# PLE gate matrix through the weight ring in place of a resident copy, with eleven row slots and three sum buffers

## What is computed

```python
for i in range(DEPTH):                    # DEPTH = 1
    ...
    h = h + merged @ w_out[i]
    h = h + peer_ffn(rms_norm(h, norm_ffn[i]), peer_wq[i], peer_keys[i], peer_u[i], peer_v[i])
    h = h + jax.nn.sigmoid(rms_norm(h, norm_ple[i]) @ ple_gate[i]) * (p[i] @ ple_proj[i])
```

## Time and profile before

| | us |
|---|---|
| three runs, median | 3986.89 |
| lowest and highest | 3982.22, 3993.07 |
| profiled execution | 3986.96 |
| its span in the profile | 3984.8 |
| PE busy in the span | 3115.6 (78%) |
| DVE busy | 2691.8 (68%) |
| ACT busy | 1377.4 (35%) |
| POOL busy | 1225.4 (31%) |

### The profile page before, as it was taken

How to read it: one execution, slowest core, us unless ns; L and a number is a source line. 1 busy time by engine, 2 the same in 40 slices (tenths; PEclk the granted TensorE clock), 3 DMA queues, 4 the chain that set the end, 5 groups by cost and what they waited for, 6 DMA issues and landing times. The chain is left out here.

```text
span 3984.8 us, 31095 instructions
## 1 busy us (share of the span) xinstructions
PE 3115.6 (78%) x7816; PEld 1412.6 (35%) x7816; DVE 2691.8 (68%) x5254; ACT 1377.4 (35%) x3574; POOL 1225.4 (31%) x1092
## 2 busy tenths in 40 slices
PE   8979999897889989878777877888765656556656
PEld 4545555543434434433333332333322222222222
DVE  3345545312477767777778777868888887888884
ACT  3213333202344344334333423343333334334332
POOL 0000000000233324433344343434444444444442
PEclk9988898798999999989889998889888878878887
DMA  4330101255899999999999999999999999999996
GB/s 160 118 141 24 44 29 37 97 209 222 349 393 414 393 360 421 418 418 378 417 398 417 361 393 391 426 355 411 424 412 399 424 419 389 420 414 393 426 422 265
DMA packets 212916, 1295.14 MB, mean 325 GB/s; under 512 B 24608, under 2 KB 38176, under 8 KB 69408
## 3 DMA queue, kind: packets, MB, share of 16 engines
q0 software_dynamic: 147456, 1073.81, 65.5%
q1 hardware_dynamic: 59552, 207.15, 13.8%
q10 hardware_dynamic: 5760, 12.59, 0.8%
HBM read 1253.60 MB, written 39.85 MB: 325 GB/s over the span
## 5 line engine op out<-in xcount | busy, mean ns | idle before, releaser
L1297 PE MATMUL l_acc<-l_rows,l_diag 128*128 128x512 f32 x2560 | 1422.6, 698 | 732.0 <-ACT l_diag L1431 718.4
L1198 POOL DMA_INDIRECT l_rows<-in_peer_uv,l_at x1024 | 1189.6, 1162 | 1732.1 <-DVE l_acc L1577 1082.3
L1567 DVE SCALAR_TENSOR_TENSOR l_rows<-l_rows,l_xn 128x1024 f32<-128x1024 f32 x1024 | 1227.1, 1224 | 320.2 <-DMA l_rows<-in_peer_uv,l_at 259.8
L1297 PEld LDWEIGHTS l_acc<-l_rows,l_diag 128*128 128x128 f32 x2560 | 526.2, 218 | 1563.6 <-ACT l_diag L1431 1025.8
L1577 DVE SCALAR_TENSOR_TENSOR l_acc<-l_rows,l_wts,l_acc 128x1024 f32<-128x1024 f32 x384 | 492.6, 1283 | 135.0 <-ACT l_wts L1427 135.0
L1423 ACT ACTIVATE l_dots<-l_dots 128x2 f32<-128x2 f32 x512 | 103.8, 203 | 1080.8 <-DVE l_rows L1567 1076.0
L1191 POOL CAST l_at<-l_expert 128x16 uint32<-128x16 f32 x64 | 35.7, 557 | 978.8 <-DVE l_expert L1553 978.5
L117 PE MATMUL l_pa<-all_ring,l_xt 128*128 128x512 f32 x656 | 296.9, 604 | 17.6 <-DMA l_xt<-kept_xnt 17.2
L117 PE MATMUL l_pa<-l_ring,l_xt 128*128 128x512 f32 x624 | 285.1, 608 | 18.2 <-DMA l_xt<-kept_xnt 12.3
L1427 ACT ACTIVATE l_wts<-l_dots,l_gates 128x1 f32<-128x1 f32 x1024 | 293.5, 287 | 16.8
L1431 ACT ACTIVATE l_diag<-all_ident,l_wts 128x128 f32<-128x128 f32 x640 | 257.1, 402 | 21.0
(11 more groups left out here) (241 smaller groups left out, 2780.4 us busy)
## 6 DMA issues: line engine op xcount, KB each, us to landing
l_ring<-in_w_late SPq DMA_DIRECT2D x44, 1024.0 KB
all_ring<-in_w_late SPq DMA_DIRECT2D x44, 1024.0 KB
l_rows<-in_peer_uv,l_at POOLq DMA_INDIRECT x1024
l_yt<-kept_yt SPq DMA_DIRECT2D x48, 256.0 KB, 12.4
kept_s<-l_yt ACTq DMA_DIRECT2D x32, 256.0 KB
l_s_in<-kept_s SPq DMA_DIRECT2D x64, 128.0 KB
mix_w_branches<-in_w_branches_kept SPq DMA_DIRECT2D x8, 768.0 KB, 4.5
kept_yt<-b_yt SPq DMA_DIRECT2D x8, 768.0 KB
```

The lines of the kernel that those rows point to most:

```text
L1198: pool.indirect_dma_start(out=rows[:, r % SLOTS, :], out_offset=None, in_=A["peer_uv"], in_offset=bass.IndirectOffsetOnAxis(ap=at[:, c % 2 ...
L1297: ins = pe.matmul(acc2[:, hs], diag[n_pe(r) % DIAGS][:], rows[:, r % SLOTS, D + half * HB:D + (half + 1) * HB], start=first, stop=last)
L1567: dve.scalar_tensor_tensor(out=u, in0=u, scalar=1.0, in1=xn[:, t % 2, :], op0=ALU.mult, op1=ALU.mult, accum_out=dots[:, n:n + 1]).then_inc ...
```

## The change

`SLOTS` goes from 8 to 11, `acc` from 2 to 3 buffers (`ACCS`), and the resident `wg` goes. In SBUF, 32 KB of each partition are given up, and 3 x 8 + 4 = 28 KB are taken. The gate matrix is appended to `w_late` as chunks 30 to 33 (two for each half), and is taken twice through the ring: once for tiles 0 and 1, between group 1 and group 2, and once for tiles 2 to 7, behind group 2. Group 2's jobs start at slot 64 x 2 + 6 = 134 rather than at 104, with the same due slot. PLE of tile t can't stand before the queries of the groups that precede its chunks (plus 4), nor before the PLE of tile t - 1 is over.

```diff
-SLOTS = 8
+SLOTS = 11
...
+ACCS = 3
+PLE_TILES = ((0, 1), (2, 3, 4, 5, 6, 7))
...
-        for g in range(len(GROUPS)):
-            self.group(g)
+        self.group(0)
+        self.group(1)
+        self.ple(PLE_TILES[0])
+        self.group(2)
+        self.ple(PLE_TILES[1])
         self.place()
-        self.ple()
...
-            begin = end
+            begin = self.first + len(PLE_TILES[0]) * NSEL // 2 + 6
         for job in rest:
+            if job.g == 2:
+                at = max(at, float(begin))
...
+    def ple(self, tiles):
+
+        c = self.take("w_late", 30, 31, 32, 33)
+        for t in tiles:
+            self.add((t,), "hturn", 1.8, pb=2, t=t)
+            for half in range(2):
+                self.add((t, half), "pgate", 6.9, pa=1, chunk=c + 2 * half, n_chunks=2, t=t, half=half)
+
+    def place_ple(self):
+
+        free = 0
         for t in range(T):
...
+            queries = [job.slot for job in self.jobs if job.kind == "query" and job.g <= (t not in PLE_TILES[0]) + 1]
+            slot = max(self.first + (t + 1) * NSEL // 2, max(queries) + 4, free)
+            self.of["hturn", t].slot = slot + 1
+            for half in range(2):
+                self.of["pgate", t, half].slot = slot + 3 + half
+            free = slot + 6
...
-        wg = sb("wg", [P, DC, D])
...
-        xn, acc = sb("xn", [P, 2, D]), sb("acc", [P, 2, D])
+        xn, acc = sb("xn", [P, 2, D]), sb("acc", [P, ACCS, D])
...
-                wait(sp, out_done, (t - 1) * 16)
-                sp.dma_start(acc[:, t % 2, :], X["h"][t]).then_inc(acc_in[t % 2], 16)
+                wait(sp, out_done, (t - ACCS + 1) * 16)
+                sp.dma_start(acc[:, t % ACCS, :], X["h"][t]).then_inc(acc_in[t % ACCS], 16)
...
-                if s == 8:
-                    sp.dma_start(wg[:], A["ple_gate"]).then_inc(wg_in, 16)
...
-                    if s == max(stored, plan.first - 1 if t < 2 else plan.first + (t - 1) * NSEL // 2 + 9):
+                    given = plan.of["pgate", t - ACCS, 1].slot + 4 if t >= ACCS else 0
+                    if s == max(stored, plan.first - 1 if t < 2 else plan.first + (t - 1) * NSEL // 2 + 9, given):
                         load_h(t)
...
-                    after = s - plan.first - (t + 1) * NSEL // 2
-                    if after == 4:
+                    if s == plan.of["pgate", t, 1].slot:
                         load_pp(t)
-                    if after == 7:
+                    if s == plan.of["pgate", t, 1].slot + 3:
                         store_tile(t)
...
-                if job.t == 0:
-                    pe.wait_ge(wg_in, 16)
+                loaded(pe, job.chunk)
+                loaded(pe, job.chunk + 1)
...
-                hs = slice(job.half * HB, (job.half + 1) * HB)
-                matmuls(pe, into_pa(job.pa[0])[:], [(ht[:, c * P:(c + 1) * P], wg[:, c, hs]) for c in range(DC)]).then_inc(pa_done, 1)
+                matmuls(pe, into_pa(job.pa[0])[:], [(ht[:, c * P:(c + 1) * P], wide_chunk(job.chunk, c)) for c in range(DC)]).then_inc(pa_done, 1)
```

More of the change, by code:

```diff
@@ L912, in place @@
         slot, used = 0, 0.0
-        jobs = iter(self.jobs)
+        jobs = iter([job for job in self.jobs if job.t is None])
         start = self.of["score", 0, 1]
@@ L940, in place @@
         self.n_slots = self.end + 10
-    def ple(self):
-        for t in range(T):
[L945 to L948, removed]
+        self.place_ple()
+    def ple(self, tiles):
[6 more added lines that the diff above has]
+        free = 0
+        for t in range(T):
+            queries = [job.slot for job in self.jobs if job.kind == "query" and job.g <= (t not in PLE_TILES[0]) + 1]
[4 more added lines that the diff above has]
+            free = slot + 6
     def searches(self):
@@ L1022, in late_stage @@
         h_out, xn_out = [sem(f"h{i}_out") for i in range(K)], [sem(f"xn{i}_out") for i in range(K)]
-        keys_in, gain_in, wg_in = sem("keys_in"), sem("gain_in"), sem("wg_in")
+        keys_in, gain_in = sem("keys_in"), sem("gain_in")
         s_out, scores_in = [sem(f"s{n}_out") for n in range(2)], [sem(f"scores{n}_in") for n in range(2)]
-        xn_in, acc_in = [sem(f"xn{n}_in") for n in range(2)], [sem(f"acc{n}_in") for n in range(2)]
+        xn_in, acc_in = [sem(f"xn{n}_in") for n in range(2)], [sem(f"acc{n}_in") for n in range(ACCS)]
         row_in = [sem(f"row{n}_in") for n in range(SLOTS)]
@@ L1136, in store_tile @@
                 sp.wait_ge(out_ready, t + 1)
-                sp.dma_start(A["out"][t], acc[:, t % 2, :]).then_inc(out_done, 16)
+                sp.dma_start(A["out"][t], acc[:, t % ACCS, :]).then_inc(out_done, 16)
             load_group(0)
@@ L1278, in turn_sum @@
                 pe.wait_ge(h2_ready, job.t + 1)
-                turn8(job, lambda c: acc[:, job.t % 2, c * P:(c + 1) * P])
+                turn8(job, lambda c: acc[:, job.t % ACCS, c * P:(c + 1) * P])
             def gate_product(job):
-                if job.t == 0:
-                    pe.wait_ge(wg_in, 16)
+                loaded(pe, job.chunk)
+                loaded(pe, job.chunk + 1)
                 for n in plan.of["hturn", job.t].pb:
                     freed_pb(pe, n)
-                hs = slice(job.half * HB, (job.half + 1) * HB)
-                matmuls(pe, into_pa(job.pa[0])[:], [(ht[:, c * P:(c + 1) * P], wg[:, c, hs]) for c in range(DC)]).then_inc(pa_done, 1)
+                matmuls(pe, into_pa(job.pa[0])[:], [(ht[:, c * P:(c + 1) * P], wide_chunk(job.chunk, c)) for c in range(DC)]).then_inc(pa_done, 1)
             def weigh(r):
@@ L1375, in norm_sum @@
                 wait(act, prms_ready, t)
-                act.activation(ht[:], acc[:, t % 2, :], ACT.Square, accum_out=prms[:, 0:1]).then_inc(prms_done, 1)
+                act.activation(ht[:], acc[:, t % ACCS, :], ACT.Square, accum_out=prms[:, 0:1]).then_inc(prms_done, 1)
                 act.wait_ge(prms_done, t + 1)
@@ L1519, in output @@
                 order(tt(o[:], o[:], ht[:], ALU.mult))
-                tt(acc[:, t % 2, :], acc[:, t % 2, :], o[:], ALU.add).then_inc(out_ready, 1)
+                tt(acc[:, t % ACCS, :], acc[:, t % ACCS, :], o[:], ALU.add).then_inc(out_ready, 1)
                 dve.wait_ge(out_ready, t + 1)
@@ L1575, in weigh @@
                 if r % NSEL == 0:
-                    dve.wait_ge(acc_in[t % 2], (t // 2 + 1) * 16)
-                dve.scalar_tensor_tensor(out=acc[:, t % 2, :], in0=rows[:, r % SLOTS, D:2 * D], scalar=wts[:, n:n + 1], in1=acc[:, t % 2, :],
+                    dve.wait_ge(acc_in[t % ACCS], (t // ACCS + 1) * 16)
+                dve.scalar_tensor_tensor(out=acc[:, t % ACCS, :], in0=rows[:, r % SLOTS, D:2 * D], scalar=wts[:, n:n + 1], in1=acc[:, t % ACCS, :],
                                          op0=ALU.mult, op1=ALU.add).then_inc(acc_done, 1)
@@ L1583, in finish @@
                 dve.wait_ge(acc2_done, n_pe((t + 1) * NSEL))
-                tt(acc[:, t % 2, :], acc[:, t % 2, :], acc2[:], ALU.add).then_inc(h2_ready, 1)
+                tt(acc[:, t % ACCS, :], acc[:, t % ACCS, :], acc2[:], ALU.add).then_inc(h2_ready, 1)
                 dve.wait_ge(h2_ready, t + 1)
@@ L1691, in layout @@
         late += quarters((np.asarray(w_proj_ret[0]), np.asarray(w_proj_sgu[0]), wpa)[br][:, cols])
-    for w_square in (np.asarray(w_out[0]), np.asarray(peer_wq[0])):
+    for w_square in (np.asarray(w_out[0]), np.asarray(peer_wq[0]), np.asarray(ple_gate[0])):
         for column in range(0, w_square.shape[1], HB):
@@ L1700, in layout @@
         "w_branches_kept": c(np.concatenate([q_a, q_r, v_s], axis=1).reshape(DC, P, KEPT * HB)), "w_branches_last": chunks(np.concatenate([u_s, g_r], axis=1)),
-        "w_late": np.stack(late), "ple_gate": chunks(ple_gate[0]),
+        "w_late": np.stack(late),
         "ple_proj": chunks(ple_proj[0]),
```

## The result

The changed kernel takes 3937.28 us (median of 4 runs, 3932.46 to 3942.75) against 3986.95 us before; the ratio is 0.9884, 95% interval 0.9866 to 0.9902. That is 50 us faster, where 3930 us (57 us faster) were forecast.

The account below looks back on a forecast made before the run. The prediction took the gather stage to be bound by nearly full DMA engines. From 3987 us, -77 (slots) + 20 (gate chunks) + 0 (planner) + 0 (waits) gave 3930 us, range 3880 to 3972 us.

Parts of the forecast that it names:

- The bound: Gather stage: DMA engines full nearly all the time (share 0.98, 401 GB/s), no compute engine full.
- Part 1: Gather stage: eleven row slots for eight cover 7.4 us of each DMA dip, gain 77 us.
- (a): Thin queue: 78 us of slow busy DMA time come largely from a nearly empty queue; half gone, 3891 us; chance 0.20.
- (b): Cover isn't rebuilt between dips, consumers set part of the tiles; half of Part 1, 3969 us; chance 0.15.
- Part 2: Gate matrix twice through the ring: eight added 1 MB chunks cost 20 us; removing the 4 MB load gives 0.
- Part 3: Planner moves group 2 and the PLE blocks of tiles 0, 2 and 3: counted 0, bound 0 to 4.5 us gain.
- Part 4: Moved waits and queues: group 2's first gate chunks have some 16 us to land, lateness 0 to 12 us, taken as 0.
- (c): Gather stage: mean rate of 401 GB/s holds, chunks cost 21 us, nothing is repaid, 4008 us; chance 0.07.
- (d): Group 2's chunks come late and PE starves at slot 134 and later chunks, 3948 us; chance 0.03.
- The wait for rows: Sign in the gather stage: DVE's wait for rows goes down from 258 to about 200 us.
- The dips behind tile ends: Sign in the gather stage: dips in DMA share behind tile ends gone or under 3 us.
- The PLE of tile 0: Sign of the planner's new order: PLE matmuls of tile 0 near 1660 us.

Follow-up runs that it names:

- late-sigmoid run of the kernel before: Kernel before, with ACT taking the sigmoid of a PLE half behind its slot's row weights instead of ahead: 3979.97 us, ratio 0.9977.
- half rows: Changed kernel, every gather but the first eleven bringing 4 KB per token in place of 8 KB, consumers' work unchanged: 3755.86 us, ratio 0.9436.

## Why the prediction was right, point by point

**The bound** was right. The DMA is full nearly everywhere, the gain came as a higher share and rate (0.99 and 411 GB/s; 0.99 was less than the 1.00 that I asked for), and PE and DVE do the same work. The bytes of q1 grew by 4.19 MB, as forecast, and the third tile, which holds slot 134, shrank. The bound does not hold in tile 0, which the consumers set.

**Part 1** (77 us) was mis-sized. The three slots are worth 0.9996 - 0.9884 = 0.0112, **45 us** (32 to 57 by the two intervals' far ends); without the gate bytes 0.0126, 50 us. The step that failed is the assumption that the queue is full again before each dip, with 7.4 us taken off every one. I took the slack as 9% everywhere, from DVE's 258 us of waiting for rows over the stage; in tile 0 it is 2%, the queue stays at a landing time of 10.2 us, and the tile got no shorter, though I had booked 7.4 us on its large dip and its small ones whole. The dip behind it, at 1450 us, reads 0.85 with eight slots and with eleven. In tile 4 the queue was full, but the stall of two PLE blocks was longer than the cover, and the tile gained 1 us. The other error went the other way: I took the slow busy time at nothing, and some of it went. Seven slots with 155 us show how large that part becomes with one slot less. With eight slots in the new order the windows' sums are 71 us idle and 140 us against 425 GB/s, so three slots took 21 us of idle and 26 us of slow busy time. So rivals (a) and (b) were each half right, and they offset.

**Part 2** (20 us) was right within the noise: 13 us with eight slots and 18 with eleven, each within some 10 us. The 0 for the removed load was not tested by itself, but the traces bound it. From the `yt` load at 812 us to the last chunk loads ahead of the gathers it is 157.9 us in the kernel before, 155.9 in the changed one, and 155.8 in the late-sigmoid run of the kernel before, which keeps the load.

**Part 3** (0, at most 4.5 us) was too low: 14 us (8 to 21). In the profile of eight slots without gate bytes, tiles 0 to 3 are 9, 14, 8 and 7 us shorter than before and tile 4 is 19 us longer. That fits three PLE blocks moved away from the group jobs and the crowd at 2800 us giving part of it back, but no run moved one block alone. I had counted only the residue that slots leave over, which is wrong with eight slots, where nothing else covers these dips. Whether the third sum buffer adds anything by itself was not tried; the order needs it.

**Part 4** (0) was right where it can be read: 16.5 us for the chunks, and no stall on PE.

**Sum.** 45 + 14 - 13 = 46 us by ratio, against 77 - 20 = 57. By medians the gain was 50 us. Part 1 was 32 us too high, Part 3 14 us and the chunks' cost 7 us too pessimistic; these offset, so that the total came within 7 to 11 us is in good part luck.

**Rivals.** (c), a fixed mean rate, is out: 401 became 411 GB/s. The memory limit of some 358 GB/s that the Trainium skill gives (page "DMA: Bandwidth & Descriptors", section "Specifications") doesn't bind here. Its row works it out as half of what a memory stack delivers, for two cores; here one core runs, so the trace says nothing of that case. Windows of 25 us at 426 to 428 GB/s agree with the 435 GB/s that the same section names as the fabric's ceiling. (d), chunks too late, did not happen.

**What would show it.** The wait for rows fell further than I said (142 for 200 us). The dips behind tile ends did not all go: the one near 1450 us stays at 0.85 though no PLE stands there any more. The jobs of group 1 make it. Ahead of its next row DVE stands for a product of such a job:

```profile
1445.42 0.69 DVE L1510 TENSOR_TENSOR l_merged<-l_pb,l_merged 128x512 f32<-128x512 f32 x1 [6.93 <-PE l_pb L117]
```

With group 1 spread over 16 more slots the same window has a share of 1.01. The PLE of tile 0 came at 1694 us, for 1660.

## What to carry to other kernels

When a transfer stream is near its ceiling, a buffer more or less is not worth "one transfer per stall". Remove one and measure: if that costs much more than adding one gives, as here (155 us for 30), the loop stands at the edge of being short of buffers in its steady state. Before counting on depth to cover stalls, measure how fast the consumers run when the stream is made cheap (here half rows), and do it stretch by stretch: where that is only a few per cent faster, the queue doesn't refill, and the next gain lies in spreading the consumers' work from tiles that they set into tiles that the stream sets.

## What the runs showed of the hardware

The DMA share hides slow busy time. With seven slots the seventh tile, which has no group jobs, read a share of 0.97 at 384 GB/s, with eleven 1.01 at 422. The share differs by 4% and the rate by 9%, so a share near 1 doesn't say that the engines run at their rate.

Depth shows up as latency. From issue to landing (tile view of the row slots) a gather took with seven and with eleven slots, and with eleven slots and half rows:

```profile
DMA to landing us min/median/max: 5.2/9.0/19.4
```

```profile
DMA to landing us min/median/max: 5.6/16.7/27.3
```

```profile
DMA to landing us min/median/max: 4.1/5.5/20.9
```

Four slots more make it 7.7 us longer in the median, where four gathers at 425 GB/s take 9.9 us. That median hides two cases. From 3000 to 3280 us the median goes from 8.8 to 17.7 us, so nearly all of the added depth stands in the queue, ready for a stall. From 1060 to 1430 us it goes from 10.0 to 10.2 us: where the consumers set the pace, four more slots add no depth at all.
